# Merged activations kept by token tile, the residual input loaded by tiles, and each expert's gate products ahead of its up products

## The chip, the cores and the metric

The kernel runs on one core of a Trainium2 chip. The metric is the device time of one execution in microseconds (us), the median of several runs. The execution that the profile describes took 1270.7 us; its instructions span 1269.0 us. Three runs without the profiler gave 1272.39, 1273.75 and 1274.04 us.

## What is computed

One layer of a decoder on 512 tokens of width 1024, in float32. A token mixer (retention heads and a gated recurrence) gives two branches, which are merged by sigmoid gates and projected; then a layer norm; then a mixture of 32 experts, of which every token uses two; then a second layer norm.

```python
merged = gate_ret * (ret @ w_ret_o) + gate_rec * (lru @ w_lru_o)
x = _layer_norm(DEEPNORM_ALPHA * x + merged @ w_out, ln1_g, ln1_b)
...
h = jax.nn.silu(xb @ w_e_gate[e]) * (xb @ w_e_up[e])
return h @ w_e_down[e]
...
return _layer_norm(DEEPNORM_ALPHA * x + moe, ln2_g, ln2_b)
```

Each expert has three matrices of 1024x512 or 512x1024: 6 MB for an expert, 192 MB for all 32, read once each.

## The kernel before

The program is written out by hand for each engine, with semaphores between them; no scheduler moves anything. Three stages matter here.

**Merging and projection.** `acc` (eight column tiles k of 128 channels by 512 tokens) becomes the merged activation. For each k ScalarE writes its rounded part `mrg_hi`, VectorE the rest `mrg_lo` (L1187 to L1189), and TensorE multiplies them with `w_out` in `project(half, t, ks)` (L1653): two column halves of 512, four token tiles t of 128 tokens. Its result is added by VectorE to the residual `x2` (L1220), which a single DMA of 2 MB brought in (L417); then comes the layer norm of tile t (`layer_norm`, L1199), for which ScalarE takes the square root (L791). In the second half, TensorE weaves the transposes of finished tiles (`turn_x2`, L1634) and their router products (`router`, L1643) into the projection. ScalarE copies each transposed tile to `x2_t` and stores the tile to DRAM (`x2t_out`, L765).

**Routing and expert 0.** When the last tile's logits are there, VectorE picks groups and experts by some thirty small operations. Meanwhile TensorE multiplies the identity by itself (`keep_warm`, L1681), which has no result that anyone reads. Then it ranks the members (L1696), picks the rows of expert 0 with a 0/1 matrix `sel` (L1703), builds the lists of tokens and weights of all experts (L1712), and transposes the picked rows (L1716). ScalarE copies between these steps (`rows_0`, `xe`, L825 and L827).

**The experts.** The expert matrices come as 192 units of 1 MB, two for each of gate, up and down, through a ring of 21 homes in SBUF (`m_raw`, MRING). SyncE issues them in order (`load_m`, L422); unit n of the first 21 waits for whoever used its home last, and from unit 21 on unit n waits for `m_done`, which TensorE raises when it has finished with a unit. The order is gate, up, gate, up for the two halves of the contraction of expert e+1, then the two down units of expert e. In `gate_up` (L1740) TensorE waits for both units of a half and multiplies: the 64 picked rows `xe` stand in the array as 64 columns, gate on columns 0 to 63 (side 0, result on PSUM partitions 0 to 63) and up on columns 64 to 127 (side 64), by turns:

```python
for k in range(4):
    for side, w in ((0, gate), (ROWS, up)):
        last = pe.matmul(bank[side:side + ROWS, 0, :], xe[:, 4 * half + k, :], w[:, FE * k:FE * k + FE], ...)
```

Between halves TensorE does the combination of the expert before last (L1789), the transposes of the next expert's rows (L1725), the down products (L1765) and the transpose of the hidden rows (L1758). After the last expert come the last combinations (L1829, L1837) and the second layer norm by tiles.

Of the kernel before, what the change touches and what calls it, by code (L numbers as in the profile page):

```python
# [130 lines left out]
def layer(nc, io, out):  # L131
    ctx = ExitStack()
    with ctx:
# [50 lines left out]
        mrg_hi, mrg_lo = at("mrg_hi", 160, [P, KD, TOKENS], F32R), at("mrg_lo", 176, [P, KD, TOKENS], F32R)  # L184
# [7 lines left out]
        m_raw = [at(f"m_raw{n}", kb, [P, 2048]) for n, kb in enumerate((80, 88, 96, 104, 112, 120, 40, 48, 56, 0, 8, 144, 152, 160, 168, 176, 184, 16, 24, 32, 192))]  # L192
# [98 lines left out]
        sel_ok, xg_clear, picked, rows_ok = (sem(n) for n in ("sel_ok", "xg_clear", "picked", "rows_ok"))  # L291
# [30 lines left out]
        def _(sp):  # L322
# [89 lines left out]
            sp.wait_ge(split_done, U_END + RING)  # L412
            sp.wait_ge(units_done, U_OUT + RING)
# [3 lines left out]
            sp.dma_start(x2[:, :, :], io["x"][0].rearrange("(t p) d -> p t d", p=P)).then_inc(res_in, 16)  # L417


            sp.wait_ge(mrg_split, KD)  # L420

            def load_m(n, src):  # L422
                if n == 9:
                    sp.wait_ge(proj_ok, TT)
                if n == 13:
                    sp.wait_ge(proj_ok, 2 * TT)
                if n == 19:
                    sp.wait_ge(x2_ok, TT)
                if n == 20:
                    sp.wait_ge(routed, TT)  # L430
                if n >= MRING:
                    sp.wait_ge(m_done, n + 1 - MRING)
                sp.dma_start(m_raw[n % MRING][:, :].rearrange("p (k n) -> p k n", k=src.shape[1]), src).then_inc(m_loaded[n % MRING], 16)
# [125 lines left out]
        def _(act):  # L559
# [194 lines left out]
            for j in range(4):  # L754
# [3 lines left out]
                for k in (2 * j, 2 * j + 1):  # L758
# [3 lines left out]
                    copy(mrg_hi[:, k, :], acc[:, k, :]).then_inc(mrg_hi_ok, 1)  # L762
# [62 lines left out]
            copy(rows_0[:, :], bank[:, 4, :]).then_inc(rows_ok, 1)  # L825
            act.wait_ge(xe_turned, 1)
            copy(xe[:, :, :].rearrange("p (h k) n -> p k h n", h=2), bank[:, 5, :].rearrange("p (k h n) -> p k h n", h=2, n=ROWS)).then_inc(xe_ok, 1)  # L827
# [46 lines left out]
        def _(dve):  # L874
# [300 lines left out]
            for j in range(4):  # L1175
# [11 lines left out]
                for k in pair:  # L1187
                    dve.wait_ge(mrg_hi_ok, k + 1)
                    sub(mrg_lo[:, k, :], acc[:, k, :], mrg_hi[:, k, :]).then_inc(mrg_split, 1)  # L1189


            dve.wait_ge(res_in, 16)
# [95 lines left out]
            def per_pick(ap, n):  # L1288
# [4 lines left out]
            dve.wait_ge(exp_ok, 2)  # L1293
            step(dve.tensor_reduce(red[:, :], exps.rearrange("p (t n) -> p t n", t=TT), AX, ALU.add))
            step.wait()
            step(dve.scalar_tensor_tensor(red[:, :], diff, 1.0, red[:, :], ALU.add, ALU.mult))
            step.wait()
            step(dve.reciprocal(wts[:, 0:TT], red[:, :]))
            step.wait()
            step(tt(wts[:, TT:2 * TT], wts[:, 0:TT], diff, ALU.mult))  # L1300

# [5 lines left out]
            tt(sel[:, :, :], iota_t[:, 1:ROWS + 1].unsqueeze(1).to_broadcast([P, TT, ROWS]),  # L1307
               place.unsqueeze(2).to_broadcast([P, TT, ROWS]), ALU.is_equal).then_inc(sel_ok, 1)
# [8 lines left out]
            tt(hot_r[:, :, :], iota_r[:, :].unsqueeze(1).to_broadcast([P, 2 * TT, ROWS]), per_pick(af[:, 0:8], ROWS), ALU.is_equal).then_inc(hot_r_ok, 1)  # L1317

# [119 lines left out]
        def _(pe):  # L1438
# [214 lines left out]
            def project(half, t, ks):  # L1653

                for k in ks:
                    if half == 0 and t == 0:
# [3 lines left out]
                        (mrg_hi[:, k, P * t:P * t + P], mrg_lo[:, k, P * t:P * t + P],  # L1660
# [28 lines left out]
            keep_warm(2)  # L1689
# [10 lines left out]
            pe.wait_ge(sel_ok, 1)  # L1700
            for t in range(TT):
                for h in range(2):
# [7 lines left out]
            for j in range(2 * TT):  # L1710
                for side in (0, ROWS):
                    last = pe.matmul(bank[side:side + ROWS, 3, 0:2 * EXPERTS], hot_r[:, j, :], ids[:, j, :], start=j == 0, stop=j == 2 * TT - 1)  # L1712
            last.then_inc(first_built, 1)
            pe.wait_ge(rows_ok, 1)
# [15 lines left out]

            def gate_up_half(half, gate, up):

                for k in range(4):
                    for side, w in ((0, gate), (ROWS, up)):
                        last = pe.matmul(bank[side:side + ROWS, 0, :], xe[:, 4 * half + k, :], w[:, FE * k:FE * k + FE],  # L1735
                                         start=half == 0 and k == 0, stop=half == 1 and k == 3)
                        if k == 3:
                            last.then_inc(m_done, 1)

            def gate_up(e, half):  # L1740
# [177 lines left out]
```

## Time and profile before

| what | value |
|---|---|
| the profiled execution, time | 1270.7 us |
| its span, first to last instruction | 1269.0 us |
| median of three runs | 1273.75 us (1272.39 to 1274.04) |
| TensorE busy | 1235.6 us, 97% |
| weight loads of TensorE | 832.1 us, 66% |
| VectorE busy | 656.9 us, 52% |
| ScalarE busy | 422.3 us, 33% |
| moved by DMA | 286.02 MB, mean 225 GB/s |
| granted TensorE clock, mean | 0.996 |

TensorE's busy time is a union of records that overlap, so 97% does not say that it runs at its best rate. Shares are averages over stages with different limits: the stages of the first 730 us move little data, the expert stage moves most of it. In the profile's rows an engine is named PE (TensorE's products), PEld (its weight loads), DVE (VectorE), ACT (ScalarE), POOL (GpSimd) or SPq (SyncE's DMA queue). L numbers are lines of the kernel.

### The profile page before, as it was taken

To read this page: it belongs to the slowest core of one execution; us is meant where nothing else is said; L and a number is where in the kernel's file an instruction comes from. 1 tells how busy PE (TensorE), PEld (TensorE's weight loads), DVE (VectorE), ACT (ScalarE), POOL (GpSimd) and SP (SyncE) were. 2 spreads that over 40 slices of the span, in tenths; PEclk is the share of its full clock that TensorE was granted. 3 is DMA by queue.
4 is the path that set the end of the run, shared out by engine and by line. 5 is a ranking of instruction groups with operands and counts; after the bars stand their busy time and mean duration, and the time that the engine had idled before them with its cause. 6 is when DMAs were issued, how large, how long until landed. Compare 5 with 4: busy or idle time off the path is not lost.

```text
span 1269.0 us, 16140 instructions
## 1 busy us (share of the span) xinstructions
PE 1235.6 (97%) x6100; PEld 832.1 (66%) x6100; DVE 656.9 (52%) x934; ACT 422.3 (33%) x600; POOL 60.9 (5%) x68
## 2 busy tenths in 40 slices
PE   7999999999999999999999999999999999998897
PEld 6888888888888888888888888333343343333332
DVE  5587765336365356347334845344454444444445
ACT  4778773223342333333343411311111111111114
POOL 0000000000000000000015100100000000000000
PEclk9999999999999999999999999999999999999999
DMA  7333322363223223223223399999999999999993
GB/s 235 108 86 96 101 66 86 95 176 93 90 67 103 86 72 100 86 66 99 83 68 99 112 407 423 361 413 404 417 418 409 416 413 415 413 418 417 413 423 163
DMA packets 143368, 286.02 MB, mean 225 GB/s; under 512 B 11733, under 2 KB 109125, under 8 KB 118736
## 3 DMA queue, kind: packets, MB, share of 16 engines
q1 hardware_dynamic: 139616, 276.81, 58.5%
q0 software_dynamic: 2544, 4.25, 1.0%
q10 hardware_dynamic: 1152, 4.19, 0.9%
q8 instruction: 38, 0.62, 0.2%
q14 instruction: 18, 0.15, 0.0%
HBM read 284.91 MB, written 4.33 MB: 228 GB/s over the span
## 4 chain that ended last, share of the span: by engine, by line
PE 87%; DMA 11%; DVE 1%; ACT 0%; SPq 0%; issue 0%; DVEq 0%; ACTq 0%
PE bank L1443 19%; PE bank L1445 19%; PE bank L1444 19%; PE bank L1735 14%; DMA m_raw<-in_w_e_up_dram 11%; PE bank L1765 6%; PE bank L1789 4%; PE bank L1725 1%; PE bank L1505 1%; PE bank L1758 1%; PE bank L1829 1%; PE bank L1574 1%; PE bank L1649 0%; DMA vec_rows<-in_b_merge_dram 0%; PE bank L1496 0%; PE bank L1498 0%
## 5 line engine op out<-in xcount | busy, mean ns | idle before, releaser
L1735 PE MATMUL bank<-m_raw,xe 128*64 128x512 f32 x1024 | 233.4, 598 | 13.8 <-DMA m_raw<-in_w_e_up_dram 13.0
L882 DVE TENSOR_TENSOR w_lo<-raw,w_hi 128x1024 fp32r<-128x1024 f32 x120 | 148.2, 1238 | 175.8 <-ACT w_hi L561 174.7
L1443 PE MATMUL bank<-xt_hi,w_hi 128*128 128x512 f32 x576 | 225.3, 391 | 0.5 <-DVE w_lo L882 0.5
L1445 PE MATMUL bank<-xt_hi,w_lo 128*128 128x512 f32 x576 | 224.2, 389 | 0.0
L1444 PE MATMUL bank<-xt_lo,w_hi 128*128 128x512 f32 x576 | 224.1, 389 | 0.0
L878 DVE TENSOR_TENSOR x<-x,bank 128x1024 f32<-128x1024 f32 x120 | 141.2, 1218 | 100.6 <-PE bank L1789 99.7
L561 ACT ACTIVATE w_hi<-raw 128x1024 fp32r<-128x1024 f32 x120 | 125.9, 1056 | 161.8 <-PE bank L1445 159.5
L1735 PEld LDWEIGHTS bank<-m_raw,xe 128*64 128x64 f32 x1024 | 71.8, 136 | 135.4 <-issue 133.0
L1443 PEld LDWEIGHTS bank<-xt_hi,w_hi 128*128 128x128 f32 x576 | 108.1, 188 | 24.1 <-issue 1.5
L1445 PEld LDWEIGHTS bank<-xt_hi,w_lo 128*128 128x128 f32 x576 | 108.1, 188 | 22.7
L1444 PEld LDWEIGHTS bank<-xt_lo,w_hi 128*128 128x128 f32 x576 | 108.2, 188 | 22.0
L1765 PE MATMUL bank<-m_raw,ht 128*64 128x512 f32 x496 | 113.5, 599 | 0.0
L811 ACT ACTIVATE h_rows<-bank 64x512 f32<-64x512 f32 x32 | 18.9, 591 | 255.5 <-PE bank L1735 255.5
L1765 PEld LDWEIGHTS bank<-m_raw,ht 128*64 128x64 f32 x496 | 32.8, 136 | 55.0 <-issue 52.9
L878 DVE TENSOR_TENSOR h_rows<-bank,h_rows 64x512 f32<-64x512 f32 x32 | 22.2, 693 | 88.3 <-ACT h_rows L811 88.2
L1789 PEld LDWEIGHTS bank<-y_hi,pick 64*128 64x128 f32 x240 | 22.4, 183 | 51.2 <-issue 48.7
L1789 PE MATMUL bank<-y_hi,pick 64*128 64x512 f32 x240 | 53.6, 443 | 0.0
L1376 DVE SCALAR_TENSOR_TENSOR y_lo<-bank,first_w,y_hi 128x512 fp32r<-128x512 f32 x31 | 23.3, 751 | 57.1 <-ACT y_hi L822 57.1
L822 ACT ACTIVATE y_hi<-bank,first_w 128x512 fp32r<-128x512 f32 x31 | 21.3, 687 | 91.4 <-PE bank L1765 91.4
L1443 PE MATMUL bank<-w_hi,xt_hi 128*128 128x512 f32 x128 | 49.8, 389 | 0.0
L1444 PE MATMUL bank<-w_lo,xt_hi 128*128 128x512 f32 x128 | 49.8, 389 | 0.0
L1445 PE MATMUL bank<-w_hi,xt_lo 128*128 128x512 f32 x128 | 49.8, 389 | 0.0
(280 smaller groups left out, 1663.4 us busy)
## 6 DMA issues: line engine op xcount, KB each, us to landing
m_raw<-in_w_e_gate_dram SPq DMA_DIRECT2D x64, 1024.0 KB, 27.6
m_raw<-in_w_e_up_dram SPq DMA_DIRECT2D x64, 1024.0 KB, 26.7
m_raw<-in_w_e_down_dram SPq DMA_DIRECT2D x64, 1024.0 KB, 27.6
raw<-in_w_in_dram SPq DMA_DIRECT2D x88, 512.0 KB, 3.8
raw<-in_w_ret_o_dram SPq DMA_DIRECT2D x16, 512.0 KB, 3.4
raw<-in_w_lru_o_dram SPq DMA_DIRECT2D x16, 384.0 KB, 3.3
raw<-in_w_out_dram SPq DMA_DIRECT2D x8, 512.0 KB, 3.7
x_rows<-in_x_dram ACTq DMA_DIRECT2D x4, 512.0 KB, 5.6
```

Source lines behind the costliest of these rows:

```text
L561: return act.activation(dst, src, ACT.Copy)
L811: act.activation(h_rows[0:ROWS, :].rearrange("q (h b p) -> q h b p", b=2, p=P), bank[0:ROWS, 0, :].rearrange("q (h p b) -> q h b p", b=2, ...
L822: act.activation(stored_rows(dst[:, :]), by_rows(bank[:, b, :]), ACT.Identity, scale=w).then_inc(yhi_ok, 1)
L878: return dve.tensor_tensor(dst, a, b, op)
L882: return dve.tensor_tensor(dst, a, b_r.bitcast(F32), ALU.subtract)
L1376: dve.scalar_tensor_tensor(stored_rows(dst[:, :]), by_rows(bank[:, b, :]), w, stored_rows(high[:, :].bitcast(F32)), ALU.mult, ALU.subtract ...
L1443: pe.matmul(dst, sh, mh, start=first and x == 0, stop=False)
L1444: pe.matmul(dst, sh, ml, start=False, stop=False)
L1445: ins = pe.matmul(dst, sl, mh, start=False, stop=last and x == n - 1)
L1735: last = pe.matmul(bank[side:side + ROWS, 0, :], xe[:, 4 * half + k, :], w[:, FE * k:FE * k + FE], start=half == 0 and k == 0, stop=half = ...
L1765: last = pe.matmul(bank[ROWS * c_:ROWS * c_ + ROWS, b, :], h[:, 2 * half + k, :], w[:, D * k + 512 * c_:D * k + 512 * c_ + 512], start=hal ...
L1789: last = pe.matmul(bank[:, (2 if t % 2 == 0 else 6) + b, :], choose[side:side + ROWS, P * t:P * t + P], y[side:side + ROWS, :], start=x == ...
```

## The change

Core of the diff; line numbers after the change are larger by up to 26. Four things are changed.

**Homes and loads.** `mrg_hi` and `mrg_lo` become `mrg[0]` and `mrg[1]`, each with two token tiles, high and low part side by side, in 160 to 176 KB and in 80 to 96 KB. The list of the ring's homes is reordered to match. Copies and differences of a column tile are now two operations of 128x256 instead of one of 128x512. `x2` comes in four DMAs of 512 KB, each as soon as its home is free.

```diff
-        mrg_hi, mrg_lo = at("mrg_hi", 160, [P, KD, TOKENS], F32R), at("mrg_lo", 176, [P, KD, TOKENS], F32R)
+        mrg = [at("mrg_01", 160, [P, 2, 2, KD, P], F32R), at("mrg_23", 80, [P, 2, 2, KD, P], F32R)]
...
-            sp.wait_ge(split_done, U_END + RING)
-            sp.wait_ge(units_done, U_OUT + RING)
+            def load_x2(t):
+                sp.wait_ge(units_done, U_RET3 + t + 1 + RING)
+                sp.dma_start(x2[:, t, :], x_view[t]).then_inc(res_in, 16)
+
+            for t in (0, 1):
+                load_x2(t)
+            sp.wait_ge(split_done, U_OUT + 6 + RING)
...
+            for t in (2, 3):
+                load_x2(t)
 
             def load_m(n, src):
+                if n == 2:
+                    sp.wait_ge(mrg_split, KD)
+                if n == 6:
+                    sp.wait_ge(split_done, U_END + RING)
                 if n == 9:
                     sp.wait_ge(proj_ok, TT)
-                if n == 13:
-                    sp.wait_ge(proj_ok, 2 * TT)
+                if 13 <= n < 17:
+                    sp.wait_ge(proj_ok, TT + n - 12)
```

**ScalarE's order.** The copy of transposed tile t-1 now stands ahead of the square root of tile t, and four idle products instead of two stand ahead of the last router.

```diff
             for t in range(TT):
+                if t:
+                    x2t_out(t - 1)
                 act.wait_ge(x2_var, t + 1)
                 act.activation(scale_v[:, 0:1], mv[:, 1:2], ACT.Sqrt).then_inc(x2_std, 1)
-                if t:
-                    x2t_out(t - 1)
...
-            keep_warm(2)
+            keep_warm(4)
             router(3)
```

**Expert 0 in parts.** VectorE's four small operations on the weights move behind `sel` and `hot_r`; `sel`, `rows_0` and `xe` are made in halves, each half with its own signal; the lists are built in two parts, three of eight ahead of the transposes and five behind.

```diff
-            tt(sel[:, :, :], iota_t[:, 1:ROWS + 1].unsqueeze(1).to_broadcast([P, TT, ROWS]),
-               place.unsqueeze(2).to_broadcast([P, TT, ROWS]), ALU.is_equal).then_inc(sel_ok, 1)
+            for half in (slice(0, 2), slice(2, TT)):
+                tt(sel[:, half, :], iota_t[:, 1:ROWS + 1].unsqueeze(1).to_broadcast([P, 2, ROWS]),
+                   place[:, half].unsqueeze(2).to_broadcast([P, 2, ROWS]), ALU.is_equal).then_inc(sel_ok, 1)
...
+            lists_part(range(3))
             for k in range(NEAR):
+                pe.wait_ge(rows_ok, 1 + k // 2)
                 last = pe.transpose(bank[:, 5, P * k:P * k + P], rows_0[:, P * k:P * k + P], ident[:, :])
             last.then_inc(xe_turned, 1)
+            lists_part(range(3, 2 * TT)).then_inc(first_built, 1)
```

**Gate ahead of up, in every expert.** The four gate products of a half are issued after a wait for the gate unit alone, then the four up products after a wait for the up unit.

```diff
+            def gate_up_part(half, side, w):
+
+                for k in range(4):
+                    last = pe.matmul(bank[side:side + ROWS, 0, :], xe[:, 4 * half + k, :], w[:, FE * k:FE * k + FE],
+                                     start=half == 0 and k == 0, stop=half == 1 and k == 3)
+                last.then_inc(m_done, 1)
...
-                n = gu_unit(e) + 2 * half
-                loaded_m(n)
-                loaded_m(n + 1)
-                gate_up_half(half, m_raw[n % MRING], m_raw[(n + 1) % MRING])
+                elif isinstance(e, int) and e == 0:
+                    pe.wait_ge(xe_rest, 1)
+                for x, side in enumerate((0, ROWS)):
+                    n = gu_unit(e) + 2 * half + x
+                    loaded_m(n)
+                    gate_up_part(half, side, m_raw[n % MRING])
```

The order in which TensorE has its instructions, from the lists of expert 0 to the end of the first half of its gate and up products. `m_raw_99` is a gate unit and `m_raw_100` the up unit of the same half. Before:

```order
L1712 MATMUL bank<-ids,hot_r 64x64 [waits hot_r_ok,ids_w_ok,ids_ok,z_ok]
L1712 MATMUL bank<-ids,hot_r 64x64 x15
L1716 MATMUL bank<-ident,rows_168 128x128 [waits rows_ok]
L1716 MATMUL bank<-ident,rows_168 128x128 x3
L1735 MATMUL bank<-m_raw_99,xe 64x512 [waits m_loaded1,m_loaded0,xe_ok]
L1735 MATMUL bank<-m_raw_100,xe 64x512
L1735 MATMUL bank<-m_raw_99,xe 64x512
L1735 MATMUL bank<-m_raw_100,xe 64x512
L1735 MATMUL bank<-m_raw_99,xe 64x512
L1735 MATMUL bank<-m_raw_100,xe 64x512
L1735 MATMUL bank<-m_raw_99,xe 64x512
L1735 MATMUL bank<-m_raw_100,xe 64x512
```

And with the change, at the same place:

```order
L1730 MATMUL bank<-ids,hot_r 64x64 [waits hot_r_ok,ids_w_ok,ids_ok,z_ok]
L1730 MATMUL bank<-ids,hot_r 64x64 x5
L1736 MATMUL bank<-ident,rows_168 128x128 [waits rows_ok] x4
L1730 MATMUL bank<-ids,hot_r 64x64 x10
L1755 MATMUL bank<-m_raw_99,xe 64x512 [waits m_loaded0,xe_ok]
L1755 MATMUL bank<-m_raw_99,xe 64x512 x3
L1755 MATMUL bank<-m_raw_100,xe 64x512 [waits m_loaded1]
L1755 MATMUL bank<-m_raw_100,xe 64x512 x3
```

Ten of sixteen list products moved behind the transposes, and gate and up, which took turns product by product, now come four by four.

ScalarE at the last two token tiles of the first layer norm. `scale_v<-mv` is the square root, `x_dram<-x_96` the store, `x_t<-bank` the copy of a transposed tile. Before:

```order
L561 ACTIVATE x_t<-bank 128x1024 [waits x2_turned]
L791 ACTIVATE scale_v<-mv 128x1 [waits x2_var]
L768 DMA x_dram<-x_96 128x1024 [waits x2_ok]
L561 ACTIVATE x_t<-bank 128x1024 [waits routed,x2_turned]
L768 DMA x_dram<-x_96 128x1024 [waits x2_ok]
L561 ACTIVATE x_t<-bank 128x512 [waits routed,x2_turned]
```

With the change:

```order
L803 ACTIVATE scale_v<-mv 128x1 [waits x2_var]
L778 DMA x_dram<-x_96 128x1024 [waits x2_ok]
L568 ACTIVATE x_t<-bank 128x1024 [waits routed,x2_turned]
L803 ACTIVATE scale_v<-mv 128x1 [waits x2_var]
L778 DMA x_dram<-x_96 128x1024 [waits x2_ok]
L568 ACTIVATE x_t<-bank 128x512 [waits routed,x2_turned]
```

The last square root moved behind the store and the copy of the tile before it.

## Rows read from the trace of the kernel before

**Rows 1.** Page, part 2: GB/s by the DMA engines in 40 equal slices
```profile
GB/s 235 108 86 96 101 66 86 95 176 93 90 67 103 86 72 100 86 66 99 83 68 99 112 407 423 361 413 404 417 418 409 416 413 415 413 418 417 413 423 163
```
**Rows 2.** Chain of waits of 1060 to 1269: start us, us, what
```profile
1205.00 26.14 DMA m_raw<-in_w_e_up_dram
...
1231.28 3.65 PE bank L1735 x16
```
**Rows 3.** Waits of PE: waited for, us in total, times, longest us
```profile
PE bank L1735 <- DMA m_raw<-in_w_e_up_dram: 13.0, 18, 1.8
```
**Rows 4.** Stretches, DMA alone: length, PEclk, DMA share, GB/s
```profile
794.00:796.00 2.00, 1.00 0.50 166
796.00:798.00 2.00, 1.00 0.42 84
```
**Rows 5.** SyncE's queue around unit 21: start us, us, engine, line
```profile
796.87 0.33 SPq L433 DMA_DIRECT2D m_raw<-in_w_e_down_dram  x1
797.25 0.43 SPq L433 DMA_DIRECT2D m_raw<-in_w_e_gate_dram  x1
```
**Rows 6.** Timeline at expert 0's first gate and up products, windows of growing length
```profile
793.20 0.65 PE L1735 MATMUL bank<-m_raw,xe 128*64 128x512 f32 x2 [0.69 <-ACT xe L561]
793.20 0.20 PEld L1735 LDWEIGHTS bank<-m_raw,xe 128*64 128x64 f32 x4 [0.93 <-ACT xe L561]
793.20 7.09 PE L1735 MATMUL bank<-m_raw,xe 128*64 128x512 f32 x32 [0.69 <-ACT xe L561]
```
**Rows 7.** Timeline at products of all 128 columns, two windows
```profile
1248.44 0.70 PE L1829 MATMUL bank<-x,ident 128*128 128x512 f32 x1
1248.44 1.98 PE L1829 MATMUL bank<-x,ident 128*128 128x512 f32 x4
```
**Rows 8.** Timeline from the third router product to the logits, PE, ACT and DVE
```profile
772.28 1.02 ACT L561 ACTIVATE x_t<-bank 128x1024 f32<-128x1024 f32 x1 [0.24 <-issue]
773.13 1.41 DVE L1212 SCALAR_TENSOR_TENSOR x<-bank,scale_v,ln 128x512 f32<-128x512 f32 x2
773.36 2.14 PE L1649 MATMUL bank<-w_rt,x_t 128*128 128x36 f32 x16 [0.85 <-ACT x_t L561]
775.31 1.95 PE L1639 MATMUL bank<-ident,x 128*128 128x128 f32 x8
777.05 1.06 PE L1684 MATMUL bank<-ident 128*128 128x128 f32 x4
777.90 2.13 PE L1649 MATMUL bank<-w_rt,x_t 128*128 128x36 f32 x16
```
**Rows 9.** Stretch of lowered clock: length, then busy (x) of PE, PEld, DVE, ACT, POOL, PEclk
```profile
775.04:778.45 3.41, 3.41 (x19) 3.41 (x18) 0.69 (x1) 1.88 (x2) 0.00 (x0) 0.50 1.00 416
```
**Rows 10.** Chain of waits of 700 to 810, transposes of an earlier tile
```profile
755.50 0.87 PE bank L1639 x8
```
**Rows 11.** Timeline from the picks to expert 0, and one copy of 256 columns
```profile
787.34 3.65 PE L1703 MATMUL bank<-x,sel 128*64 128x512 f32 x16
...
790.82 1.10 PE L1712 MATMUL bank<-ids,hot_r 128*64 128x64 f32 x32
791.04 0.60 ACT L561 ACTIVATE rows<-bank 128x512 f32<-128x512 f32 x1 [5.79 <-PE bank L1703]
791.85 0.66 PE L1716 MATMUL bank<-ident,rows 128*128 128x128 f32 x4
792.55 0.60 ACT L561 ACTIVATE xe<-bank 128x512 f32<-128x512 f32 x1 [0.91 <-PE bank L1716]
802.92 0.38 ACT L561 ACTIVATE ht<-bank 128x256 f32<-128x256 f32 x1 [1.36 <-PE bank L1758]
```
**Rows 12.** Timeline, VectorE's first step behind the projection
```profile
739.23 0.69 DVE L1220 SCALAR_TENSOR_TENSOR x<-x,bank 128x512 f32<-128x512 f32 x1 [8.07 <-DMA x<-in_x_dram]
```
**Rows 13.** The gather for expert 1: its issue in the timeline, its landing by tile
```profile
793.89 1.03 POOL L524 DMA_INDIRECT xg<-x_dram,first_x  x1 [0.29 <-POOL xg L530]
...
DMA to landing us min/median/max: 3.7/3.7/3.7
```

More of the change, by code:

```diff
@@ L761, in _ @@
                     act.wait_ge(turned, 4 * HEADS + 4)
-                    copy(mrg_hi[:, k, :], acc[:, k, :]).then_inc(mrg_hi_ok, 1)
+                    act.wait_ge(acc_ok, KD)
+                    for side in range(2):
+                        last = copy(mrg[side][:, :, 0, k, :], acc[:, k, 256 * side:256 * side + 256].rearrange("p (t n) -> p t n", t=2))
+                    last.then_inc(mrg_hi_ok, 1)
             assert nxt == U_END
@@ L824, in _ @@
             act.wait_ge(picked, 1)
[L825 removed]
+            for half in range(2):
+                copy(rows_0[:, 256 * half:256 * half + 256], bank[:, 4, 256 * half:256 * half + 256]).then_inc(rows_ok, 1)
             act.wait_ge(xe_turned, 1)
[L827 removed]
+            for half, ok in enumerate((xe_ok, xe_rest)):
+                copy(xe[:, 4 * half:4 * half + 4, :], bank[:, 5, :].rearrange("p (k h n) -> p h k n", h=2, n=ROWS)[:, half, :, :]).then_inc(ok, 1)
             act.wait_ge(x2_stored, 16 * TT)
@@ L1188, in _ @@
                     dve.wait_ge(mrg_hi_ok, k + 1)
-                    sub(mrg_lo[:, k, :], acc[:, k, :], mrg_hi[:, k, :]).then_inc(mrg_split, 1)
-            dve.wait_ge(res_in, 16)
+                    for side in range(2):
+                        last = sub(mrg[side][:, :, 1, k, :], acc[:, k, 256 * side:256 * side + 256].rearrange("p (t n) -> p t n", t=2), mrg[side][:, :, 0, k, :])
+                    last.then_inc(mrg_split, 1)
+            dve.wait_ge(res_in, 16 * TT)
             dve.wait_ge(ln1_ordered, 1)
@@ L1709, in _, with lists_part @@
             pe.wait_ge(ids_w_ok, 1)
[L1710 to L1714, printed above, removed]
+            def lists_part(js):
+                for j in js:
+                    for side in (0, ROWS):
+                        last = pe.matmul(bank[side:side + ROWS, 3, 0:2 * EXPERTS], hot_r[:, j, :], ids[:, j, :], start=j == 0, stop=j == 2 * TT - 1)
+                return last
+            lists_part(range(3))
             for k in range(NEAR):
+                pe.wait_ge(rows_ok, 1 + k // 2)
                 last = pe.transpose(bank[:, 5, P * k:P * k + P], rows_0[:, P * k:P * k + P], ident[:, :])
             last.then_inc(xe_turned, 1)
+            lists_part(range(3, 2 * TT)).then_inc(first_built, 1)
             def turn_x(s):
@@ L1729, in loaded_m @@
                 pe.wait_ge(m_loaded[n % MRING], 16 * (n // MRING + 1))
-            def gate_up_half(half, gate, up):
[L1733 to L1738, printed above, removed]
+            def gate_up_part(half, side, w):
[3 more added lines that the diff above has]
+                last.then_inc(m_done, 1)
+            def gate_up_half(half, gate, up):
+                gate_up_part(half, 0, gate)
+                gate_up_part(half, ROWS, up)
             def gate_up(e, half):
```

26 lines of the change are left out of this document (12 added, 14 removed).

## The prediction

> **What bounds the kernel now.** I read the page first. From about 730 us on the DMA engines move some 415 GB/s in every slice but one, which has 361 [rows 1]. That is the whole expert stage. Then the chain of waits at its end: pieces of DMA alternate with short pieces of gate and up products, and the last such wait ends at 1231.2; from 1231.28 on the chain is TensorE's to the end, 37.7 us [rows 2]. In the waits, TensorE stood still for expert weights 18 times, 13.0 us in all, each time for an up unit, the later one of a half [rows 3]. So the expert stage is paced by the stream of 192 units, and TensorE would need 13.0 us less for it.
>
> What sets the stream's position in time? In the slice with 361 it nearly stops: 166 and 84 GB/s between 794 and 798 [rows 4]. All 21 homes are full by then, and unit 21 leaves at 796.87, unit 22 at 797.25 [rows 5]: both wait for the first gate and up products, which began at 793.20 [rows 6]. From there 171 units follow without a gap that matters. The end of the kernel is therefore tied to the **start of expert 0's products**, 793.20, plus the 3.67 us to the first release. Everything that shifts this moment shifts the end by as much, as long as the homes are full by then. Anything that only fills the homes sooner gives nothing.
>
> **The change, part by part.** Times are against the profiled execution: span 1269.0, its own time 1270.7, which is 3.05 us under the median of 1273.75. I put the difference on the median.
>
> *Homes and loads.* `x2` comes in parts as homes come free, two units leave ahead of the merged activations, and four of the ring's units leave one by one during the projection instead of together behind it. VectorE's wait of 8.07 us for `x2` [rows 12] goes, but among TensorE's waits none names VectorE or `x2` in the projection: the largest in the expert stage is the one of rows 3, and from 731 to 769 there is none. The ring fills some 8 us sooner and then stands still longer. Worth 0. The two-part copies of `mrg` cost ScalarE about 0.14 us for a column tile more (two copies of 256 columns at 0.38 against one of 512 at 0.60 [rows 11]) and VectorE about as much, sixteen operations more in all, some 2.4 us together, on engines that wait in that stretch, since TensorE has the first six column tiles of two token tiles to do before it needs the last two. If that cover went, the last of them would come about 1 us late; I count 0.
>
> *ScalarE's order.* The copy of transposed tile 2 began at 772.28, behind a square root, and TensorE waited 0.85 us for it ahead of its router product at 773.36 [rows 8]. Now it can start when the transposes are done, and the wait goes. What is late next is the last tile of the layer norm: VectorE ends it at 773.13 + 1.41 = 774.54 [rows 8], so the last transposes start at about 774.6 instead of 775.31: -0.7. The square roots of tiles 1 to 3 now queue behind a copy of 1.0 us; the one of tile 2 comes about 1.9 us later and holds VectorE about 1 us, in front of an idle time that is longer than that.
>
> *Four idle products instead of two.* The granted clock was 0.50 of full, that is 1.2 GHz, from 775.04 to 778.45, after low-density router work with a pause in it [rows 9]. The eight transposes took 1.74 us (775.31 to 777.05) and the two idle products 0.85 (to 777.90), 2.59 us in all [rows 8]. With four of them at 1.2 GHz all the way: 1.74 + 1.70 = 3.44, +0.85. With the clock at 2.4 GHz: 0.87 for the transposes as for an earlier tile [rows 10] and 0.85 for the products, 1.72, -0.87. With the fall at the same moment as before it lies between, about +0.4. No row tells which, since the work in front becomes denser by less than 1 us. I take the middle, 0.0, and keep both ends. Router and logits follow unchanged.
>
> *Expert 0 in parts.* `sel` comes 0.3 us sooner, but the four idle products ahead of the picks keep TensorE until then anyway (the row of 787.34 has no idle time in front [rows 11]): at most -0.1. Behind the picks the row was: copy of `rows_0` 0.60 to 791.64, sixteen list products to 791.85, transposes, copy of `xe` 0.60 to 793.15 [rows 11]. Now the first half copy (0.38, the `ht` copy's size [rows 11]) ends at about 791.4, transposes run to about 792.1, the first half of `xe` is there at about 792.5, and the ten list products (1.10 us for sixteen) fill that gap on TensorE. Products start at about 792.6: -0.6, bounds -0.7 (all of the copies' halves) and 0 (if list products and transposes stand in each other's way). The gather for expert 1 starts about 0.9 us later against the products; it landed 3.7 us after 793.89 and was wanted at 800.2 [rows 13, 6], so 2.6 us of slack cover it.
>
> *Gate ahead of up.* The same 16 products in a half, in another order. Each is two records in the profile: 16 rows of the order for two halves, 32 records in 7.09 us [rows 6]. A product of all 128 columns runs its records one after another: four in 1.98 us [rows 7]. With 64 columns two run **side by side**, gate on one half of the array and up on the other: at 793.20 two records start together, four weight loads within 0.20 us [rows 6]. One pair takes 7.09/16 = 0.44 us, a lone record with 128 columns 1.98/4 = 0.49. The two that start together cannot be the two of one product, which share their columns, so TensorE takes up's first record ahead of gate's second: it looks ahead past at least one record. In the new order it has to look past eight records of gate and their eight weight loads. If it does, the two streams still run together, and the part costs nothing; in the DMA-paced stretch gate products start when their own unit lands, but the up products then need their 8 x 0.43 us alone, so a half ends as before, perhaps 0.2 us sooner: -0.2 once, after the last wait.
>
> *The sum*: -0.7 + 0.0 - 0.1 - 0.6 - 0.2 = **-1.6 us**, bounds -0.7 - 0.9 - 0.1 - 0.7 - 0.2 = -2.6 and -0.7 + 0.85 + 0 = +0.2. So 1269.1 for a profiled execution, **1272.1** for the median, own range 1270 to 1275 with the spread of the runs.
>
> **The rivals.**
>
> *Gate and up one after another (slower).* If TensorE does not look past gate's eight records, nothing stands beside them and each half needs 16 steps instead of 8: 8 x 0.43 = 3.44 us more. In 64 halves that is 220 us. TensorE then paces the stage and its 13.0 us of waiting vanish: 1273.75 + 220 - 13 - 1.6 = about 1479. If it looks past some of them, up starts when, say, six steps of gate are over: 6 x 0.43 x 64 = 165, about 1424. It decides from the point at which up starts more than 13.0/64 = 0.2 us behind gate. For it: no row of before has more than two records of one column half in succession with work for the other half behind them. Against it: the records that started together show that order alone does not bind. The Trainium skill, "TensorE: Matmul & The Clock Gate", Part 3 (packing small matmuls), says that weight loads may be pulled forward in a window of 64 instructions, but that matmuls keep strict program order. By that rule the time would be this rival's; taken strictly the trace already contradicts it, as up's first record could not have started with gate's first.
>
> *The clock falls elsewhere.* If the low clock moves onto the picks, these 3.65 us [rows 11] cost up to that much more, and the gains before them are used up: 1273.75 - 1.6 + 3.6 = about 1275.8, and with a part of it about 1274.
>
> *The loads matter after all.* If the stream's place were set by its beginning, 8 us sooner would show: 1273.75 - 8 = 1266. Against it, the stop at 794 to 798 [rows 4].
>
> **How the numbers follow.** Forecast 0.70; one after another 0.19; the clock 0.09; the loads 0.02. 0.2% of 1273.75 is 2.55 us, about what a measurement of this kernel can tell from no change. The forecast's centre lies inside it; about a third of its cases go past -2.55, through the clock: faster 0.24 + 0.02 = 0.26. Slower: 0.19 + 0.02 of the clock = 0.21. The rest, 0.53, is no change. The range of 1269.8 to 1276.0 holds the forecast and the clock case, some 0.79; the case of 1424 to 1479 is left out as a whole.
>
> **What would show it.** Right: `up` records that start with `gate` records, 7.1 us for a first pair of halves; expert 0's first product at about 791.6, unit 21 about 3.7 us behind it; waits for up units still near 13 us; no wait ahead of the router product of tile 2. Wrong: weight loads of one column half alone at every 0.43 us, no wait for DMA in the expert stage, under 400 GB/s there; or a first product that is not sooner; or a stream that does not stop at the full ring.

## The result, and the profile after

The changed kernel takes **1365.42 us** (median of 4 runs, 1363.91 to 1366.17) beside 1273.07 us for the kernel before on the same chip (4 runs): a ratio of 1.0728, 95% interval 1.0706 to 1.0750, so 92 us slower. The profiled execution took 1363.9 us with a span of 1362.2. The forecast was 1272.1, the range 1269.8 to 1276.0. The kernel came out slower, as the rival "gate and up one after another" had it, though far below that rival's 1424 and 1479.

From the page of the changed kernel: TensorE, the GB/s in 40 slices, the largest group of instructions, and the loads of the expert units with their median from issue to landing.

```profile
PE 1341.9 (99%) x6104; PEld 868.8 (64%) x6104; DVE 657.2 (48%) x943; ACT 422.6 (31%) x610; POOL 61.1 (4%) x68
...
GB/s 224 95 110 80 91 78 93 159 100 102 63 108 77 77 92 92 62 108 77 78 116 363 419 284 392 375 365 365 376 370 373 367 373 363 373 373 369 319 34 62
...
L1755 PE MATMUL bank<-m_raw,xe 128*64 128x512 f32 x1024 | 343.1, 599 | 0.0
...
m_raw<-in_w_e_gate_dram SPq DMA_DIRECT2D x64, 1024.0 KB, 8.9
```

The two lines of the page of before that answer to the last two:

```profile
L1735 PE MATMUL bank<-m_raw,xe 128*64 128x512 f32 x1024 | 233.4, 598 | 13.8 <-DMA m_raw<-in_w_e_up_dram 13.0
...
m_raw<-in_w_e_gate_dram SPq DMA_DIRECT2D x64, 1024.0 KB, 27.6
```

The same 1024 records of gate and up, of the same length (599 and 598 ns), now keep TensorE busy for 343.1 us instead of 233.4, since fewer of them run side by side. The DMA queue is no longer the pace: 363 to 392 GB/s in the expert stage instead of some 415 [rows 1], a unit lands 8.9 us after its issue instead of waiting 27.6 in a queue, and in the last slice but one the stream is already over (34 GB/s). TensorE's waits (waited for: us in total, times, longest us) say the same; there is no `m_raw` among them any more:

```profile
PE bank L1487 <- DMA vec_rows<-in_b_merge_dram: 8.7, 1, 8.7
PE bank L1784 <- DVE h_rows L890: 1.3, 1, 1.3
PE bank L1458 <- DVE w_lo L894: 1.1, 1, 1.1
PE bank L1654 <- DVE x L1226: 0.3, 1, 0.3
PE bank L1458 <- DVE mrg L894: 0.2, 1, 0.2
```

The balance of the two spans: 343.1 - 233.4 = +109.7 us of gate and up, -13.0 for the waits that went [rows 3], -2.2 because expert 0's first product came at 791.00 instead of 793.20 [rows 6]. That makes +94.5; the spans differ by 93.2.

How the lost overlap looks: the weight loads at expert 0's first half, in the timeline of the changed kernel (start us, us, engine, line, operation, how many in this row).

```profile
790.95 0.20 PEld L1755 LDWEIGHTS bank<-m_raw,xe 128*64 128x64 f32 x2
...
791.44 0.14 PEld L1755 LDWEIGHTS bank<-m_raw,xe 128*64 128x64 f32 x1 [0.29 <-issue]
791.87 0.14 PEld L1755 LDWEIGHTS bank<-m_raw,xe 128*64 128x64 f32 x1 [0.29 <-issue]
792.30 0.14 PEld L1755 LDWEIGHTS bank<-m_raw,xe 128*64 128x64 f32 x1 [0.29 <-issue]
792.72 0.19 PEld L1755 LDWEIGHTS bank<-m_raw,xe 128*64 128x64 f32 x3 [0.29 <-issue]
```

Before, four loads stood at the very start [rows 6]: two for gate, two for up. Now there are two, then one every 0.43 us, which is gate alone, and only at 792.72 three together: up has begun. The first product is at 791.00, so up starts 1.72 us behind gate, which is **four steps of 0.43 us**: neither with gate (the forecast) nor after gate's eight records. When up starts, gate's fifth record starts and three stand behind it. A half that stands by itself took this long in the chain of waits of the changed kernel:

```profile
822.45 5.35 PE bank L1755 x16
827.80 1.13 PE bank L1815 x8
828.93 0.49 PE bank L1746 x8
829.41 3.58 PE bank L1791 x16
833.00 0.39 PE bank L1784 x4
833.39 5.35 PE bank L1755 x16
```

5.35 us is 12.4 steps of 0.43. Side by side it would be 8, one after another 16.

### The profile page after: what moved, and what is told of

It reads as the page before. It is cut to its first block, busy times and chain, and to the rows that moved or that the text cites. A ratio compares the mean times of both kernels' runs of the same rounds, so it can differ in the third digit from the quotient of the medians.

```text
span 1362.2 us, 16115 instructions
## 1 busy us (share of the span) xinstructions
PE 1341.9 (99%) x6104; PEld 868.8 (64%) x6104; DVE 657.2 (48%) x943; ACT 422.6 (31%) x610; POOL 61.1 (4%) x68
## 4 chain that ended last, share of the span: by engine, by line
PE 96%; DVE 2%; ACT 1%; issue 0%; DMA 0%; SPq 0%; DVEq 0%; ACTq 0%
PE bank L1755 25%; PE bank L1458 17%; PE bank L1460 17%; PE bank L1459 17%; PE bank L1791 8%; PE bank L1815 5%; PE bank L1746 1%; PE bank L1784 1%; DVE wo_lo L894 1%; PE bank L1520 1%; PE bank L1699 1%; PE bank L1855 1%; PE bank L1589 1%; DMA vec_rows<-in_b_merge_dram 0%; PE bank L1511 0%
## 5 line engine op out<-in xcount | busy, mean ns | idle before, releaser
L1755 PE MATMUL bank<-m_raw,xe 128*64 128x512 f32 x1024 | 343.1, 599 | 0.0
L1755 PEld LDWEIGHTS bank<-m_raw,xe 128*64 128x64 f32 x1024 | 110.4, 137 | 191.2 <-issue 189.1
L531 POOL DMA_INDIRECT xg<-x_dram,first_x x31 | 29.2, 942 | 479.1 <-PE bank L1746 478.8
L1460 PE MATMUL bank<-ret_hi,w_lo 128*128 128x512 f32 x128 | 49.8, 389 | 0.0
```

The lines of the kernel that those rows point to most:

```text
L531: pool.indirect_dma_start(xg[0:ROWS, :], None, x2_dram, bass.IndirectOffsetOnAxis(ap=idx, axis=0), bounds_check=last_x, oob_is_err=False). ...
L1460: ins = pe.matmul(dst, sl, mh, start=False, stop=last and x == n - 1)
```

## The experiments

Three theories stood at the start. **A, a limited look-ahead:** TensorE takes up work for the other column half as long as no more than three records wait ahead of it. **B, the wait in the middle:** the semaphore wait for the up unit, which the change puts between gate and up, holds up back. **C:** the loss comes from other parts of the change, such as homes, loads or expert 0 in parts. All ratios are against the kernel before on the same chip, with their 95% interval. It was run again beside the experiments, 23, 35 and 17 times, with medians of 1273.97, 1273.05 and 1273.42 us.

### 1. Turns kept, the rest of the change kept

```diff
                 for k in range(4):
-                    last = pe.matmul(bank[side:side + ROWS, 0, :], ...)
+                    for side, w in ((0, gate), (ROWS, up)):
+                        last = pe.matmul(bank[side:side + ROWS, 0, :], ...)
```

> The changed kernel with one part undone: gate and up products take turns again, product by product, both waits for units ahead of them. Everything else of the change stays. Theory A (up's products start only when no more than three records of gate still wait ahead of them): the halves go back from 5.35 us to 3.58 us, the waits for up units return (13 us or more, each below 2 us), and since expert 0's first product comes at about 791.0 instead of 793.2, the time is 1273.1 - 2.2 = about 1270.9 (1269.5 to 1272.5). Theory C (the loss comes from the homes, the loads, or expert 0 in parts): the time stays near 1365.

Measured: 1270.58 us (12 runs), ratio 0.9978 (0.9963 to 0.9994). The whole loss is gone and 2.8 us with it. TensorE waits for up units again, 12.9 us in 16 times, and an isolated half takes 3.58 us in the chain of waits. C falls.

```profile
818.62 3.58 PE bank L1759 x16
```

### 2. Gate and up four by four, alone

```diff
-                for k in range(4):
-                    for side, w in ((0, gate), (ROWS, up)):
+                for side, w in ((0, gate), (ROWS, up)):
+                    for k in range(4):
```

> The kernel before with one edit: in each half four gate products, then four up products, both waits for units still ahead of all eight. Theory A (look-ahead of three waiting records): up starts 4 steps of 0.43 us behind gate, a half takes 5.3 us, and the time is 1273.1 + 64 x 1.75 - 13 (waits that go) - 2 (tail hidden) = about 1368 (1364 to 1373). Theory B (the wait for the up unit, which stands in the middle in the changed kernel, is what keeps up back): the time is that of before, 1273. Theory C (other parts of the change): also 1273.

Measured: 1368.31 us (two runs, 1365.78 and 1370.84), ratio 1.0743 (1.0713 to 1.0773). The order of the eight products alone makes the loss, with both waits ahead of all. B falls as its cause, and the size is A's, in the time and in the isolated half of 5.35 us. The weight loads in the timeline of this kernel show the same four steps, 791.40 to 793.17:

```profile
791.40 0.19 PEld L1738 LDWEIGHTS bank<-m_raw,xe 128*64 128x64 f32 x2 [0.92 <-ACT xe L561]
791.89 0.14 PEld L1738 LDWEIGHTS bank<-m_raw,xe 128*64 128x64 f32 x1 [0.29 <-issue]
...
793.17 0.19 PEld L1738 LDWEIGHTS bank<-m_raw,xe 128*64 128x64 f32 x3 [0.29 <-issue]
```

### 3 to 5. How far it looks: groups of two, three and one, two and four and two

The first edit; the others replace the list of groups by `((0, 1, 2), (3,))`, and by up 0, 1, gate 0 to 3, up 2, 3.

```diff
-                for k in range(4):
+                for ks in ((0, 1), (2, 3)):
                     for side, w in ((0, gate), (ROWS, up)):
+                        for k in ks:
```

> As the kernel with turns kept, but two gate products, two up products, two gate, two up; both waits ahead. Each product is two records, so ahead of up's first record stand four records of gate, of which three wait when the first has started. Theory A (work for the other column half starts with up to three records waiting ahead of it): nothing is lost, 3.6 us for a half, the time of the kernel with turns kept (within 1 us of it, 1271). Rival A1 (only one record may wait, the other half of the same product): up starts two steps late in each half, 4.4 us for a half, 1271 + 64 x 0.87 - 13 = about 1314.

> As the kernel with turns kept, but three gate products, three up, one gate, one up; both waits ahead. Theory A (three waiting records): six records of gate, up starts when the third starts, two steps of 0.43 us late, and the same two steps stand at the end: 4.4 us for a half and 1271 + 64 x 0.87 - 13 = about 1314 (1308 to 1318). Rival A1 (one waiting record): four steps late, 5.3 us, about 1368. Rival A2 (no look-ahead limit, a fixed loss at four in a row alone): 1271.

> As the kernel with turns kept, but in each half two up products, then four gate products, then two up; both waits ahead. Four of one column half stand in a row as in the changed kernel, but the other half's work stands on both sides. Theory A (work for the other column half starts with up to three records waiting ahead of it): gate's first record stands behind four records of up, three waiting: it starts with them. Up's third product stands behind eight records of gate and starts when five of them have started, at step 4, just when up's first four records are through. Nothing is lost: 3.6 us for a half, about 1271. Rival A2 (four products of one column half in a row cost their time wherever they stand): 5.3 us for a half, about 1368.

| order in a half | isolated half | time, us | ratio |
|---|---|---|---|
| by turns | 3.58 us | 1270.58 | 0.9978 (0.9963 to 0.9994) |
| groups of two | 3.63 us | 1270.37 | 0.9973 (0.9961 to 0.9984) |
| up 2, gate 4, up 2 | 3.65 us | 1269.98 | 0.9970 (0.9954 to 0.9987) |
| three and one | 4.49 us | 1311.85 | 1.0300 (1.0274 to 1.0326) |
| four and four | 5.35 us | 1368.31 (experiment 2) | 1.0743 (1.0713 to 1.0773) |

The halves in the chains of waits of these three kernels, in the table's order:

```profile
818.84 3.63 PE bank L1759 x16
```

```profile
818.18 3.65 PE bank L1756 x16
```

```profile
816.45 4.49 PE bank L1759 x16
```

A gave 3.6, 3.6 and 4.4 us and 1271, 1271 and 1314. A look-ahead past one record alone would have cost the groups of two 43 us. Two or four waiting records do not fit either: up would start three steps late or one in the order of three and one, and 4.49 - 3.58 = 0.91 us is two steps of 0.43. The order of two, four, two has four gate products in a row as the changed kernel has, and costs nothing: not the length of a run matters, but how many records wait ahead of the first one of the other half.

### 6. The wait in the middle by itself

```diff
                 n = gu_unit(e) + 2 * half
                 loaded_m(n)
-                loaded_m(n + 1)
...
+                        if side and ks[0] == 0:
+                            loaded_m(n + 1)
```

> As the kernel with groups of two, but the wait for the up unit stands behind the first two gate products instead of ahead of all, as in the changed kernel it stands between gate and up. Theory A: the wait's place costs nothing when the unit is there; 3.6 us for a half, 1270.4 as with both waits ahead, within 1 us; the waits of TensorE for up units keep their number, those of the last stretch shorter by at most 0.9 us each. Theory B (a wait in the middle keeps what is behind it from being looked at until gate's records are through): up starts 3 to 4 steps late, 4.9 to 5.3 us, 1340 to 1368.

Measured: 1270.51 us, ratio 0.9980 (0.9965 to 0.9995), an isolated half of 3.63 us. The wait costs nothing in its place. TensorE's waits for up units shrank to 0.7 us, once, from 9.0 us in 12 times in experiment 3; that their number would stay, as was expected, was wrong. The first two gate products stand in that time now: gate and up keep TensorE busy for 246.3 us instead of 236.1. The time did not follow, since the stream paces the stage and not TensorE.

### 7. Does the limit count records or products?

In float32 each product is two records. With the upper two bytes of each value read as bfloat16 it is one, so that four products are four records and three of them wait. These two kernels leave out the lower bits of `xe` and of the gate and up weights.

```diff
-                    last = pe.matmul(..., xe[:, 4 * half + k, :], w[:, FE * k:FE * k + FE], ...)
+                    last = pe.matmul(..., xe[:, 4 * half + k, :].bitcast(BF16)[:, 1::2],
+                                     w[:, FE * k:FE * k + FE].bitcast(BF16)[:, 1::2], ...)
```

> Turns kept, but gate and up read only the upper two bytes of each value, as bfloat16, so that each product is one record instead of two. This leaves out the lower bits of xe and of the gate and up weights. It is the measure for the next run. Expected: a half takes 8 records in pairs, 4 steps, about half of 3.58 us, 1.8 us or less; the expert stage waits for DMA instead, so the time says little: 1262 to 1271.

> The same bfloat16 products, four gate and then four up. Ahead of up's first record stand four records, three waiting when the first has started. Theory A (the limit counts waiting records): nothing is lost, a half takes as long as with turns. Rival A3 (the limit counts products, one and a half of them): up starts when the third gate product starts, two steps late, so a half takes 6 steps instead of 4, half as long again. Rival A2 (four products in a row cost their time): 8 steps, or 6.5, clearly longer than A3's bound of the turns.

Expert 0's first two halves and a later half that stands by itself, in the timelines, by turns and then four by four:

```profile
793.24 1.98 PE L1759 MATMUL bank<-m_raw,xe 128*64 128x512 bf16 x16
...
816.66 1.09 PE L1759 MATMUL bank<-m_raw,xe 128*64 128x512 bf16 x8
```

```profile
792.83 2.01 PE L1759 MATMUL bank<-m_raw,xe 128*64 128x512 bf16 x16
...
816.74 1.10 PE L1759 MATMUL bank<-m_raw,xe 128*64 128x512 bf16 x8
```

The two orders take the same time, 1.09 and 1.10 us for the 8 records of a half. The rival that counts products wanted six steps there instead of four, some 1.6 us. So four products of one half in a row are harmless when they are four records. It is records that count and not products, or something that goes with records. Two such things no run separates: each record has one weight load, and a bound in time (three waiting float32 records are 3 x 0.43 = 1.29 us of work, three of bfloat16 less) would pass all these kernels too. The times, one execution each, were 1269.69 and 1271.45 us. TensorE's gate and up work fell from 233.4 to some 93 us and its waits for up units rose to 102.5 and 97.5: taking 140 us from TensorE bought nothing, because the stream is the bound at turns. The mean granted clock of these two executions was 0.939 and 0.933, the lowest of all here, and their times show no loss by it. The other direction costs, as experiments 2 and 4 show, once the 13 us of slack are used up.

### 8. The other parts: idle products, homes, and the kernel before again

> As the kernel with groups of two, with two idle products ahead of the last router product instead of four. In the stretch from the last transposes to the router product, four idle products took 1.83 us at the full clock in the changed kernel (774.71 to 776.54), two took 1.35 in the grouped kernel (774.94 to 776.29). Expected: the first expert product 0.4 to 0.9 us sooner against the start of the third set of transposes at the same clock (21.1 us to about 20.7 where the clock does not fall, 22.5 to about 21.8 where it falls), 1270.4 - 0.5 = about 1269.9. If the idle products are what keeps the clock up, the clock falls here and the time is the same or 1 us more.

> The kernel before with the homes and loads of the change, and nothing else: mrg by token tiles, x2 in four loads, the ring's homes reordered, units 2, 6 and 13 to 16 with the change's waits. ScalarE's order, the two idle products, expert 0 in one piece and the turns are those of before. The prediction put this at 0.0: then 1273.1 to 1274, and the stream stops longer at the full ring (6 us near zero GB/s ahead of unit 21). If loads matter: 1266. If the whole gain of the kernel with turns kept (ratio 0.9978) came from here, the ratio is 0.998 and the distance from the third set of transposes to expert 0's first product stays at 23.4 us (21.9 with the full clock).

> The kernel before with two of the change's parts, ScalarE's order and expert 0 in parts; homes and loads, the turns of gate and up, and the two idle products are those of before. If the homes and loads of the change cost what the traces show (from the first product of the projection to the third set of transposes 47.6 us with them, 47.1 without), this kernel's first expert product comes 67.9 us behind the first product of the projection where the clock does not fall (47.1 + 20.75), against 68.3 with the homes of the change, and the time is that of the kernel with groups of two and two idle products less 0.5: about 1268.6. If the homes and loads bring part of the gain of 2.8 us (a ratio of 0.9978 with turns kept, where the traces account for 0.3 at the same clock), the time is between that kernel's and 1273: 1270 to 1272.

> The kernel before, unchanged, for a second profile. Ahead of expert 0 its clock fell in the first profile, and did not in the kernel before with gate and up grouped, whose program is the same up to there; so the fall is chance and not order. Expected: 23.4 us from the third set of transposes to the first expert product if the clock falls as before, 21.9 if it does not, more if it falls for longer; 475.8 us from that product to the end in each case, within 0.7.

The edit of the first is `keep_warm(4)` to `keep_warm(2)` ahead of `router(3)` in the kernel with groups of two; the second is the first block of the change's diff on the kernel before; the third is its second and third block without the four idle products.

| kernel | time, us | ratio | projection to third transposes | from there to expert 0's first product | from there to the end |
|---|---|---|---|---|---|
| before | 1273.07 | 1 | 47.13 | 23.44 | 475.80 |
| before, again | 1270.86 (one run) | | 47.12 | 24.89 | 474.56 |
| four by four alone | 1368.31 | 1.0743 | 47.09 | 21.87 | |
| homes and loads alone | 1272.74 | 0.9984 (0.9966 to 1.0001) | 47.62 | 28.15 | 475.09 |
| the change | 1365.42 | 1.0728 | 47.59 | 21.12 | |
| turns kept | 1270.58 | 0.9978 | 47.56 | 22.42 | 475.69 |
| groups of two, two idle products | 1269.10 | 0.9975 (0.9959 to 0.9990) | 47.62 | 20.75 | 475.53 |
| homes kept | 1269.12 | 0.9976 (0.9960 to 0.9993) | 47.16 | 20.75 | 476.42 |

The last three columns are differences of row starts in each kernel's timeline: first product of the projection, third set of transposes (769.76 before, 769.88 in the changed kernel), first gate product, span. Two expectations were missed. The kernel before, again, took 474.56 us from expert 0's first product to the end, where 475.8 within 0.7 was expected. In "homes and loads alone" the stream stood longer than the expected 6 us (0 GB/s from 790 to 800), as the first product came late. The columns show three things.

*The homes cost 0.46 us on the path, and no run shows it in time.* Every kernel with the new homes takes 47.6 us for the projection up to there, every one with the old 47.1; the wait for `mrg` of 0.2 in the waits above is a part of it. Yet "homes kept" (1269.12) is not faster than its counterpart (1269.10), though 0.5 us less was expected (1268.6). A reason may be that with the old homes and a first product at 790.58 the ring is not full in time: the stream still runs when the homes come free, while with the new ones it stands. The stretches of the kernel with homes kept, then of the one with groups of two and two idle products (length; busy of PE, PEld, DVE, ACT, POOL; PEclk, DMA share, GB/s):

```profile
792.00:794.00 2.00, 2.00 (x12) 0.59 (x10) 1.75 (x14) 2.00 (x3) 1.07 (x2) 1.00 0.94 397
794.00:796.00 2.00, 2.00 (x12) 0.72 (x10) 1.86 (x6) 1.77 (x2) 0.00 (x0) 1.00 0.80 217
```

```profile
792.00:794.00 2.00, 2.00 (x12) 0.91 (x10) 1.83 (x14) 2.00 (x3) 1.65 (x2) 1.00 0.03 8
794.00:796.00 2.00, 2.00 (x12) 0.82 (x9) 1.78 (x7) 1.98 (x3) 0.00 (x0) 1.00 0.49 119
```

The way from the first product to the end is 476.42 us there and 475.53 here. That this is the reason stays unproven: over the nine float32 profiles that the stream paces, this way lies anywhere from 474.5 to 476.4 us.

*Where the stream stands, the end follows the first product, within that scatter.* In the run of "homes and loads alone" the first product came at 798.91, 5.7 us later than before, and the span was 1274.0, 5.0 longer. In the second profile of the kernel before it came 1.4 us later than in the first, and the span was 0.2 us longer.

*The same program runs with and without the fall of the clock.* The delay in "homes and loads alone" has one cause: in this execution the clock was at half, 1.2 GHz, for some 13.6 us (each stretch below by how far its mean is under 1.00) and not for 3.4 as in [rows 9]:

```profile
773.00:778.00 5.00, 4.15 (x25) 4.04 (x25) 2.50 (x4) 1.07 (x2) 0.00 (x0) 0.71 0.99 369
778.00:784.00 6.00, 6.00 (x30) 6.00 (x29) 1.25 (x4) 1.88 (x2) 0.00 (x0) 0.50 1.02 423
784.00:788.00 4.00, 4.00 (x21) 4.00 (x20) 3.45 (x18) 0.00 (x0) 0.00 (x0) 0.50 1.00 410
788.00:790.00 2.00, 2.00 (x17) 2.00 (x17) 1.79 (x10) 0.22 (x1) 0.00 (x0) 0.82 0.15 61
```

With ScalarE's old order, which leaves the pause of 0.85 us among the router products, the clock fell in three of four profiles, and cost 1.6, 3.0 and 6.3 us against the fourth (21.87). With the new order it fell in five of ten, and cost 1.3 to 1.7 against the others (21.12 with four idle products). The kernel before and the four-by-four one run the same program up to expert 0, and one fell and one did not. So a single profile cannot price this stretch.

The order is not without effect on it, though. Each execution on record has the mean granted clock of its whole span. It was 0.993 or less in 38 of the 76 executions of the kernel before that stand beside the experiments and in 6 of the 12 of "homes and loads alone", but in only 6 of the 64 with the new order on ScalarE and expert 0 in parts (experiments 1, 3, 5 and 6, two idle products, homes kept). The time goes with it: the kernel before took 1276.0 us on average at 0.991 (12 executions) and 1270.3 at 0.997 (11). A straight line common to all these kernels gives 0.98 us for each 0.001, and at equal clock it leaves turns kept 0.4 us faster than the kernel before, plus or minus 0.7. This is an estimate from the record: the mean says how much of the low clock there was and not where.

## Why the prediction was wrong, point by point

**What bounds the kernel: right for before.** The bfloat16 kernels show it best (less TensorE work, same time), and "homes and loads alone" shows the tie to expert 0's first product, which holds to within a microsecond or two and not "by as much".

**Homes and loads, 0: too low on the path by 0.46 us.** The path through the projection became longer by that much, where "I count 0" stood; a wait for the two-part `mrg` of 0.2 us is a part of it. In time no run shows it (ratio 0.9984, 0.9966 to 1.0001).

**ScalarE's order, -0.7: right.** The pause ahead of the third router product went, and the last tile of the layer norm is what is late next, as said. From the third to the last transposes it took 4.83 us in the changed kernel (769.88 to 774.71) against 5.55 before (769.76 to 775.31), or 5.41 in the four-by-four kernel, which runs the same order (769.53 to 774.94).

```profile
769.88 1.04 PE L1654 MATMUL bank<-ident,x 128*128 128x128 f32 x8
770.75 3.66 PE L1664 MATMUL bank<-w_rt,x_t 128*128 128x36 f32 x32
774.71 1.09 PE L1654 MATMUL bank<-ident,x 128*128 128x128 f32 x8 [0.30 <-DVE x L1226]
775.64 1.06 PE L1699 MATMUL bank<-ident 128*128 128x128 f32 x8
776.54 1.87 PE L1664 MATMUL bank<-w_rt,x_t 128*128 128x36 f32 x16
```

**Four idle products, 0.0 between -0.87 and +0.85: right as bounds, wrong as an effect of the edit.** In the changed kernel the clock stayed at 2.4 GHz and transposes and idle products took 1.83 us (774.71 to 776.54) instead of 2.59. But with two idle products it was quicker still, 20.75 against 21.12 us to the first product. Where the clock fell it took 3.11 us with turns kept (775.13 to 778.24). Which of the two came varied from one execution to the next. Both profiles with two idle products and the new order kept the clock up, against three of eight with four, too few to tell.

**Expert 0 in parts, -0.7 with `sel`: nearly right.** At the same clock the way from the picks to the first product fell from 5.86 us (785.54 to 791.40, four by four alone) to 5.41 (785.59 to 791.00), -0.45 where -0.6 stood; from the idle products to the picks it fell from 1.18 us (784.36 to 785.54) to 1.07 (784.52 to 785.59), -0.1 as said. The first product was forecast for about 791.6 and came at 791.00.

**These parts together, -1.4.** The kernel with turns kept is 2.8 us faster (0.8 to 4.7), so the range held for it. At the same clock the traces account for -0.75 + 0.46 = -0.3. The rest is luck, as far as the prediction goes, since its middle gave the clock no gain. It fits a clock that falls less with the new order: in the fourteen profiles 2.7 us are lost on average with the old order and 0.7 with the new, and the line through the executions above leaves 0.4 us at equal clock. Why the new order helps the clock is not shown.

**Gate ahead of up, -0.2 ("the part costs nothing"): here it failed.** The step read [rows 6] rightly as far as it went: "TensorE looks ahead past at least one record. In the new order it has to look past eight records". Then it priced the new order at nothing for TensorE, and gave 0.70 to a look-ahead of eight, for which there was no row, beside one of which the trace showed a single record. Experiments 2 to 5 measure three waiting records. From that the step comes out by its own arithmetic: up starts four steps late in each half, 4 x 0.43 x 64 = 110 us, less the 13.0 us of waits: about 1369, where 1365 and 1368 were measured. The rival had the mechanism, its point of decision (0.2 us behind gate) and the end of the waits right; "say, six steps" was a number without a row, and its 1424 stood too high. The range left the case out as a whole. With one record shown and eight needed, the two ought to have had their chances the other way round.

**The rule.** The measurements contradict a strict order of matmuls: with it an isolated half four by four would take at least the 15 steps until up's last record, 6.5 us, and it took 5.35; three and one took 4.49. In time, seven steps late in each half are 7 x 0.43 x 64 = 193 us more, an estimate of some 1452, where 1365.42 was measured. The Trainium skill, "TensorE: Matmul & The Clock Gate", Part 3, states strict order, and this case's runs do not agree for two column halves. The prediction was right that the rule does not hold to the letter, and wrong to put 0.70 on a look-ahead that nothing bounds. The rule's direction was the useful part of it.

**What would show it.** The first three signs for "wrong" came true: weight loads of one half alone every 0.43 us, no wait for an expert unit, under 400 GB/s. The other two, a first product that is not sooner and a stream that does not stop, did not.

## A faster version

Turns kept with the rest of the change is faster than before by 0.22% (0.06 to 0.37). Groups of two with two idle products stands at 0.9975, the up 2, gate 4, up 2 order at 0.9970, old homes with the new order on ScalarE and in expert 0 at 0.9976. Their intervals overlap; no run tells which is best. All beat both kernels. What they have in common is the new order on ScalarE and expert 0 in parts; homes and loads alone have a ratio whose interval reaches 1.0001. Most of the 2.8 us of turns kept goes with the clock that fell less, by the estimate above.

## What to carry to other kernels

Products that are to run side by side on two column halves must stand close to each other in the program: here, with no more than three records of the one half waiting ahead of the other's next, counting two records for a float32 product. That was measured for halves of 64 columns and records of 512. An order can be priced before it runs, by giving each record one step and letting the other half start only under that limit. And where a trace shows a mechanism at a depth of one and the change needs a depth of eight, that is a guess and not a reading; the cheap test is the reordered loop alone.

## What was not expected of the hardware

- The look-ahead over matmuls reaches past three waiting records and no further: halves of 3.58, 3.63, 3.65, 4.49 and 5.35 us for five orders of the same 16 records. Where two halves follow each other with nothing between them, as expert 0's first two, the loss comes once: 1.83 us together (8.92 against 7.09), and not twice 1.77, since gate's second half starts while up's first still runs.
- The granted clock fell at the same place in three of four executions of one order of the program and in five of ten of another, and in the old order for 3.4, some 6.8 or some 13.6 us, with the same instructions in front.
- A semaphore wait in the middle of the products, for a unit that is already there, did not hold the look-ahead back (3.63 us for a half with it and without it).
